# Three mixture-of-experts layers: routing joined to the experts, and token rows packed in 21 blocks instead of 24

## The reference, cut to what matters

```
logits = h @ w_group + b, h @ w_expert + b
group  = best of 4;  experts = best 2 of the 8 in it;  gates from both softmaxes
for each expert e, for the rows that chose it:
    y = (silu(x @ w_gate[e]) * (x @ w_up[e])) @ w_down[e]
out[token] = sum over its two rows of gate * y
```

## Time and profile before

| | us |
|---|---|
| median of 3 runs | 4115.12 (4114.41 to 4116.6) |
| the profiled execution, its own time | 4115.45 |
| its span from first to last instruction | 4113.5 |
| PE busy | 3484.4 (85%) |
| DVE, ACT, POOL busy | 1571.3, 873.8, 235.5 |
| bytes moved by DMA | 842.26 MB, 205 GB/s in the mean |

### The profile page before, as it was taken

One profiled execution on the slowest core, in us unless ns is written; L12 is line 12 of the kernel. 1 busy time (PEld: TensorE's weight loads), 2 busy tenths in 40 slices (PEclk: granted clock), 3 DMA queues, 4 the chain that ended last, 5 costly groups with the idle time before them and its releaser, 6 DMA issues. The chain is left out here.

```text
span 4113.5 us, 48036 instructions
## 1 busy us (share of the span) xinstructions
PE 3484.4 (85%) x18756; PEld 1936.0 (47%) x18756; DVE 1571.3 (38%) x2595; ACT 873.8 (21%) x1896; POOL 235.5 (6%) x250
## 2 busy tenths in 40 slices
PE   7998988499999598999874999985999657847994
PEld 3444644144444244777442444433556456425662
DVE  4641755200000674666452000004426673551114
ACT  0001721011111123555110101002335322001112
POOL 1002000200000100000002000001000000011001
PEclk9999998699999799999986999997999878968997
DMA  9963031599996610000316999956210310419994
GB/s 379 357 220 122 7 130 66 209 427 426 426 422 256 201 57 1 1 1 2 140 56 239 427 426 427 421 227 213 88 46 23 112 46 22 159 36 366 420 390 195
DMA packets 176908, 842.26 MB, mean 205 GB/s; under 512 B 53455, under 2 KB 60367, under 8 KB 130610
## 3 DMA queue, kind: packets, MB, share of 16 engines
q1 hardware_dynamic: 142434, 737.83, 44.8%
q0 software_dynamic: 20576, 54.16, 3.6%
q10 hardware_dynamic: 13680, 47.24, 2.9%
HBM read 758.39 MB, written 97.20 MB: 208 GB/s over the span
## 5 line engine op out<-in xcount | busy, mean ns | idle before, releaser
L395 PE MATMUL front_acc<-front_hT,front_wt 128*128 128x512 f32 x512 | 224.8, 601 | 5.5 <-DMA front_wt<-in_na_w_qkv 5.5
L1215 PE MATMUL n_acc<-n_wt,n_hT 128*128 128x512 f32 (+2 forms) x512 | 191.3, 531 | 0.7 <-ACT n_hT L1255 0.7
L201 DVE TENSOR_REDUCE gqa_top<-gqa_scores 128x1 f32<-128x1024 f32 x128 | 150.8, 1220 | 101.5 <-PE gqa_scores L149 101.5
L232 ACT ACTIVATE gqa_probs<-gqa_scores,gqa_top 128x1024 f32<-128x1024 f32 x128 | 142.5, 1113 | 168.2 <-DVE gqa_top L201 168.2
L2137 PE MATMUL m1x_gp<-m1x_w,m1x_xT 128*128 128x512 f32 (+1 forms) x512 | 171.9, 600 | 1.5 <-issue 0.7
L2137 PE MATMUL m0x_gp<-m0x_w,m0x_xT 128*128 128x512 f32 (+1 forms) x512 | 171.4, 599 | 1.5 <-issue 0.7
L2162 PE MATMUL m1x_yp<-m1x_w,m1x_hidT 128*128 128x512 f32 (+1 forms) x512 | 169.3, 594 | 2.1 <-ACT m1x_hidT L2223 2.1
L2162 PE MATMUL m0x_yp<-m0x_w,m0x_hidT 128*128 128x512 f32 (+1 forms) x512 | 169.3, 594 | 2.1 <-ACT m0x_hidT L2223 2.1
L2137 PE MATMUL m0x_up<-m0x_w,m0x_xT 128*128 128x512 f32 (+1 forms) x512 | 168.8, 593 | 0.0
L2137 PE MATMUL m1x_up<-m1x_w,m1x_xT 128*128 128x512 f32 (+1 forms) x512 | 168.8, 593 | 0.0
L913 PE MATMUL n_acc<-n_wt,n_hT 128*128 128x512 f32 x384 | 168.2, 598 | 0.7 <-ACT n_hT L931 0.7
(11 more groups left out here) (617 smaller groups left out, 5469.6 us busy)
## 6 DMA issues: line engine op xcount, KB each, us to landing
m0x_w<-in_moe_w_gate SPq DMA_DIRECT2D x32, 2048.0 KB, 33.3
m0x_w<-in_moe_w_up SPq DMA_DIRECT2D x32, 2048.0 KB, 33.2
m0x_w<-in_moe_w_down SPq DMA_DIRECT2D x32, 2048.0 KB, 33.4
m1x_w<-in_moe_w_gate SPq DMA_DIRECT2D x32, 2048.0 KB, 32.7
m1x_w<-in_moe_w_up SPq DMA_DIRECT2D x32, 2048.0 KB, 32.7
m1x_w<-in_moe_w_down SPq DMA_DIRECT2D x32, 2048.0 KB, 33.2
v<-in_ada_w SPq DMA_DIRECT2D x40, 1024.0 KB, 12.4
m2x_w<-in_moe_w_gate SPq DMA_DIRECT2D x32, 1024.0 KB, 32.2
```

What stands on the lines that cost most here:

```text
L201: dve.tensor_reduce(top[:, n % 2, h:h + 1], scores[h][:, :], AX.X, ALU.max, negate=True).then_inc(max_ready, 1)
L232: act.activation(probs[:, n % 2, h], scores[h][:, :], ACT.Exp, bias=top[:, n % 2, h:h + 1], accum_out=total[:, n % 2, h:h + 1]).then_inc(p ...
L395: last = pe.matmul(acc[n % 4][:, :], wt[:, c % 2, k, i * P:(i + 1) * P], hT[:, k, half * 512:(half + 1) * 512], start=k == 0, stop=k == KC ...
L1215: last = pe.matmul(acc[c][:, 0:n1 - n0], hT[:, t % 2, k], wt[:, k, n0:n1], start=k == 0, stop=k == KC - 1)
```

## The change

`route` and `experts` become one stage, `mixture`. What it does, part by part:

- Logits stay in SBUF (`keep["raw"]`); the store and the load go. Identity, router constants, token numbers and biases are loaded once, at the end of `front`, and stay; the identity loads in the other stages go. `tri`, `ones` and a new table `across` are loaded at the stage's start.
- Counts come from one reduction and two matmuls; experts are ranked with a 32 x 32 comparison; the list of experts by rank is a matmul (`plan_ps`), and SP starts the weights from it.
- The list of rows for the gathers is made on chip: a 2048-element comparison per partition on DVE, 16 matmuls that make a table (expert x position), and 8 matmuls that pick the blocks' columns out of it. The first two gathers are issued from it.
- The places of the rows in HBM (`place_rows`, 20 DVE operations up to `places`), the 16 indirect DMAs and the stores of places and gates remain, but now behind gathers 0 and 1 on POOL's queue and ahead of gather 2; on DVE they stand behind the first copy of the transposed rows. They serve overflow blocks and the next stage.
- Packing: the 16 smallest experts stay two to a block with 64 rows each (8 blocks). The next 12 (ranks 16 to 27) get 96 rows each: nine have a block's first 96 rows, and three are cut in pieces of 32 rows that fill the rest of three blocks each (9 blocks). The four largest have 128 (4 blocks). 21 blocks, and 22 in m2.
- A piece of 96 rows is done as 64 + 32, so in each of the nine blocks every step has three matmuls, with array tiles of 64, 32 and 32 columns, in that order.
- The weight ring of 10 slots becomes a table of 9 (18 in m2), each slot given to the matrix whose slot is free earliest; a cut expert's three matrices stay for three blocks.
- `SPILL_BLOCKS` goes from 16 to 21.

```diff
-SPILL_BLOCKS = 16
+SPILL_BLOCKS = 21
...
+        self.cap = [HALF_P] * SMALL + [96] * (LONE + SPLIT) + [P] * (R - top0)
+        self.cap[-1] += P * tops
...
+        pair = [(i, [(2 * i, 0, HALF_P), (2 * i + 1, HALF_P, HALF_P)]) for i in range(pairs)]
+        lone = [(pairs + i, [(SMALL + i, 0, 96), (split0 + i // SPLIT, 96, 32)]) for i in range(LONE)]
+        large = [(pairs + LONE + i, [(top0 + i, 0, P)]) for i in range(R - top0)]
...
+        def pieces(n):
+            out = []
+            for r, row, width in layout.blocks[n][1]:
+                while width:
+                    size = P if width == P else min(width, HALF_P)
+                    out.append((r, slice(row, row + size)))
+                    row, width = row + size, width - size
+            return out
...
                         for k in range(KC):
-                            for s, q in enumerate(qs):
-                                r = rows_of(n, s)
-                                last = pe.matmul(acc[r, 0:F], xT[:, j, k, r], w[:, q % RING, k * F:(k + 1) * F], start=k == 0, stop=k == KC - 1)
+                            for r, part in pieces(n):
+                                last = pe.matmul(acc[part, 0:F], xT[:, j, k, part], w[:, place_of[m_, r][0], k * F:(k + 1) * F],
+                                                 start=k == 0, stop=k == KC - 1)
...
+                pool.wait_ge(d, at["rows"])
+                gather(0)
+                gather(1)
+                pool.wait_ge(filled, 16)
+                pool.wait_ge(d, at["places"])
+                for k in range(2):
+                    for t in range(T):
+                        pool.indirect_dma_start(out=row_table, ...).then_inc(t_st, 16)
+                pool.dma_start(places, pu[:, :, :]).then_inc(out_st, 16)
+                gather(2)
...
+                choose()
+                rank_experts()
+                list_rows()
+                copy_x(dve, dve.tensor_copy, 0, 0)
+                place_rows()
+                weigh_rows()
+                product(0)
...
-                sp.wait_ge(l_cp, TILES)
-                sp.dma_start(rows(logits), lg[:, :, :]).then_inc(l_st, 16)
-                sp.wait_ge(l_st, 16)
```

More of the change, by code:

```diff
@@ L335, in _ @@
                 load_weights(5)
+                for tile, src in keep["loads"]:
+                    sp.dma_start(tile, src).then_inc(kept_in, 16)
+                sp.wait_ge(kept_in, 16 * len(keep["loads"]))
             @block.gpsimd
@@ new lines, with mixture @@
+SMALL = 16
+def mixture(nc, name, keep, bt, constants, h, wg, wu, wd, y, layer, row_table, places, gates, layout):
+    F = wg.shape[-1]
+    KC, FC = D // P, F // P
+    UNIT = KC * F
+    RING = layout.slots
+    G, E, T, X = N_GROUPS, PER_GROUP, TILES, N_EXPERTS
+    by_expert = lambda w: w.rearrange("l e (p c) f -> (l e) p (c f)", p=P)
+    sources = {"g": by_expert(wg), "u": by_expert(wu), "d": by_expert(wd)}
+    LAYERS_EXPERTS = wg.shape[0] * X
+    place_of, N, LISTED = layout.place, layout.N, layout.listed
+    ROWS = N + SPILL_BLOCKS
+    BASE = N * P
+    ident, cst, raw, tok_id = (keep[n] for n in ("ident", "cst", "raw", "tok_id"))
@@ new lines, in mixture @@
+        tri, ones, across = (sb(n, [P, P]) for n in ("tri", "ones", "across"))
+        empty = sb("empty", [P, ROW_BLOCKS], U32)
+        ri, rcol = sb("ri", [P, ROWS], U32), sb("rcol", [P, 1], U32)
+        x, xT = sb("x", [P, 2, D]), sb("xT", [P, 2, KC, P])
+        w = sb("w", [P, RING, UNIT])
+        sg, hid, hidT, yt = sb("sg", [P, 2, F]), sb("hid", [P, 2, F]), sb("hidT", [P, FC, P]), sb("yt", [P, 2, D])
+        at_pos = yt[:, :, :].rearrange("p e (n q) -> p (e n) q", q=P)
+        turn = [st.ps(f"turn{b}", [P, 512]) for b in range(2)]
@@ L1842, in _ @@
[L1842 to L1870, removed]
@@ new lines, in _ @@
+                for n_ in range(1, N):
+                    product(n_)
+                    if n_ + 1 < N:
+                        copy_x(dve, dve.tensor_copy, n_ + 1, 0)
+                    copy_y(dve, dve.tensor_copy, n_ - 1, 0)
+                copy_y(dve, dve.tensor_copy, N - 1, 0)
+                dve.sem_inc(so_y[0], 1)
+                spills = spilled(dve)
+                for j in range(2):
+                    dve.wait_ge(stored[j], 16 * ((N + 1 - j) // 2))
+                with dve.Fori(0, SPILL_BLOCKS) as i:
+                    with dve.If(i < spills):
+                        dve.wait_ge(so_t, i + 1)
+                        dve.tensor_copy(xT[:, 0, half[0]], turn[0][:, :].rearrange("p (c s) -> p c s", c=4)).then_inc(so_cp[0], 1)
+                        dve.wait_ge(so_sg, i + 1)
+                        dve.tensor_tensor(hid[:, 0], sg[:, 0], up[0][:, 0:F], ALU.mult).then_inc(so_hid, 1)
+                        dve.wait_ge(so_st, i * 16 + 16)
+                        dve.wait_ge(so_dn, i + 2)
+                        dve.tensor_copy(yt[:, 0, 0:512], yp[0][:, :]).then_inc(so_y[0], 1)
@@ L2150, in down @@
                 def down(n):
[L2151 to L2153 removed]
+                    arrived("d", n)
                     if n:
@@ L2983, in host_constants @@
     moe = [np.arange(N_GROUPS, 0, -1), np.arange(PER_GROUP, 0, -1), P * np.arange(TILES), np.arange(N_EXPERTS)]
-    moe = np.concatenate([np.tile(np.concatenate(moe), (P, 1)), part[:, None]], axis=1)
+    moe = [np.tile(np.concatenate(moe), (P, 1)), part[:, None], part[:, None] + P * np.arange(TILES)[None, :] - UNUSED_ROW]
+    for tops in range(2):
+        layout = Layout(tops, 18)
+        moe += [np.pad(np.array(v), (0, P - N_EXPERTS))[:, None] for v in (layout.start, layout.cap, layout.stair)]
+    moe = np.concatenate(moe, axis=1)
     return {
@@ L2999, in build, with stages @@
 def build(nc, a, out):
+    with ExitStack() as stack:
+        tile = lambda n, shape, dt=F32: stack.enter_context(nc.sbuf_tensor(f"keep_{n}", shape, dt))
+        keep = {"ident": tile("ident", [P, P]), "cst": tile("cst", [P, a["moe_const"].shape[1]]),
+                "tok_id": tile("tok_id", [P, TILES], U32), "raw": tile("raw", [P, TILES, N_GROUPS + N_EXPERTS]),
+                "bias": [tile(f"bias{i}", [P, N_GROUPS + N_EXPERTS]) for i in range(3)]}
+        stages(nc, a, out, keep)
+def stages(nc, a, out, keep):
     def scratch(name, *shape, dt=F32):
```

593 lines of the change are left out of this document (303 added, 290 removed).

## The result

The changed kernel takes **4531.95 us** (median of 4 runs, 4527.66 to 4533.83) against 4115.86 for the kernel before (4 runs, 4114.41 to 4117.07): ratio 1.1011, 95% interval 1.0997 to 1.1024. The forecast was 4497, so +382 against a measured +416. The profiled execution took 4527.66 us with a span of 4525.9, 4 us under the median.

What follows compares the result with a forecast made beforehand. PE was taken to bound the mixture stages, DMA just behind. m0 and m1 at -68 + 234 - 33 + 9 + 3 = +145 each and m2 at +92 gave +382 on 4115.4, about 4497 us; range 3890 to 4540.

Steps and rivals of the forecast that it cites:

- The mixed step: Nine mixed blocks: 64 then 32s, drained between, 1.94 us a step; +234 us in m0 and m1, +134 in m2; chance 0.62.
- Side by side: Rival, mixed blocks: 64- and 32-column pieces overlap, a step stays 0.86 us, DMA decides m0 and m1; 3923 us; chance 0.28.
- In turn without draining: Rival, mixed blocks: groups of 64 and 32 follow at the stream's pace, 1.72 us a step; 4360 us; chance 0.07.
- staggered: Rival, mixed blocks: each piece starts a pass after the one before, 1.29 us a step; about 4123 us; chance 0.03.
- Three blocks fewer: Blocks of each mixture stage: three fewer at an unchanged price save 68 us in m0 and m1, 36 in m2.
- The head: Stage start, logits to first product: the first product comes 32.8 us earlier, 30 in m2.
- Gather 2: After PE's first blocks: rows of gather 2, issued behind the scatters, come late; cost 9 us in m0 and m1, 21 in m2.
- The tail: Last store to next stage: five more empty turns of the overflow loop, +3 us a layer.

Runs made afterwards that it cites:

- e1: Changed kernel with a lone expert's 96 rows as three pieces of 32 columns instead of 64 + 32; 3943.04 us, 0.9581 of the kernel before.
- e2: Changed kernel with, in mixed blocks, all steps of the 64-column piece before all steps of the two 32s; 4382.79 us, ratio 1.0648.
- e6: Changed kernel without the third piece of each mixed block, leaving one tile of 64 and one of 32 columns a step; 4530.6 us, one run.
- e3: Changed kernel with the packing of the kernel before (no mixed blocks, 16 overflow turns); 4052.93 us, ratio 0.9848.
- e4: Changed kernel with gather 2 issued ahead of the 16 scatters; 4489.27 us.
- e5: Changed kernel with the 96 rows as three pieces of 32 and gather 2 ahead of the 16 scatters; 3945.52 us, ratio 0.958.
- e8: Changed kernel with pieces of 32 and the overflow loop inside one test, gather 2 behind the scatters; 3913.4 us, ratio 0.9507.
- e9: e8 with gather 2 first and the scatters spread, four ahead of each of gathers 3 to 6; 3891.23 us, ratio 0.9456.

## Why the prediction was right, and where its terms were off

**The mixed step** was the step that decided, and it held: forecast 1.94 us a step with bounds 1.90 and 1.98, measured 15.88 / 8 = 1.985. I had taken the middle; the upper end, two fenced groups of 0.99 as in the earlier trace rows, was the measurement. The e1 block of 22.9 against 49.7 makes +26.8 a block instead of +26.0, +241 instead of +234 in m0 and in m1. In m2 a gate step is 9.05 / 8 = 1.13 (forecast 1.09); with down 8.01 against 3.65 a block costs 2 x (9.05 - 3.51) + 4.36 = 15.4, nine +139 instead of +134. (By its own terms the forecast's width of 35 us for 1.90 to 1.98 a step is that of m0 and m1 alone; m2's 180 mixed steps add 14. And its 703 us of PE should be 477 + 234 = 711.) That nothing overlaps across widths, which the earlier trace rows showed only at hand-overs, e2 and e6 show inside a step. The Trainium skill (TensorEngine Tiling (Array Packing), section Key Properties) says that a change of tiling mode drains TensorE. The trace agrees, and adds the size, 0.11 to 0.13 us a change here, against 6.89 us a product for the lost overlap.

**Side by side**, the rival at 0.28, is refuted for unequal tiles and confirmed for equal ones: e1 lands at 3943 where that rival gave 3923, with the DMA engines as the limit, as it was worked out. The Trainium skill (TensorE: Matmul & The Clock Gate, section Measured speedup vs the span model) gives packed tiles the span of one matmul and some 4 ns for each further tile. For four tiles of 32 the trace agrees (6.89 us a product), for 64 beside 32 it doesn't (14.00 at best). **In turn without draining** would give 8 x 1.72 = 13.8 us a gate product and is refuted by 15.88, and by the 1.88 us between e2 and the changed kernel; **staggered** would give 10.3, and is refuted by 15.88 and by e6.

**Three blocks fewer**: -68 and -36 were right while PE ends the stage. With cheap mixed blocks they aren't: from e3 to e1 m0's part shortens by 1321.6 - 1278.6 = 43 us, or 46 with the 3.5 of five more turns taken off; about 22 of 68 are lost. Waits for weights are 13.3 of them, and the up products behind the two longest are 3.9 longer than usual (8.47 and 9.53 us for 7.05; granted clock 0.83 and 0.74). The two kernels' own difference doesn't see that.

**The head**: weights start at 722.65 (forecast 722.6). The list was there at 733.5 instead of 737.7, because the small float32 products were mis-sized, 10.8 us for 48 records: the 32 of the table took 5.54 us, 0.173 each, and the 16 that pick from it 1.0, lying side by side in the trace. So the first product came at 747.85 instead of 752.3, -37.1 instead of -32.8; in m2 (4005.71 - 3965.35 = 40.4 after the logits against 76.6) -36.2 instead of -30.

**Gather 2**: waits of 8.55 us in m0 and 17.7 in m2 against 9 and 21. Missing was what follows a pause: the next down product took 9.17 us instead of 7.03, 2.1 us more, at a granted clock of 0.76.

**The tail**: 3.7 us instead of 3.

In m0 the measured terms are -37.1 - 68 + 241 + 8.6 + 2.1 + 3.7 = +150 of 158. Another 1.6 us is the first product (10.13 against 8.54 us, at a granted clock of 0.70 in 748 to 758 us against 0.84 in 785 to 794), 2.6 the second block, whose gate and up products took 16.57 us in this execution and 13.95 in those of e2 and e4. Some 4 us are left, 2 of them because a mixed block is 27.0 us above the 22.7 of the kernel before. The layers of m0 and m1 were forecast 13 and 16 us short, m2 2 us: mixed blocks and slow starts were priced too low, and the head's gain too low as well, which partly cancels.

**Left open**: what holds ACT and DVE in m2 while the scatters run, and breaks the second up product in all three layers. The changed kernel and e5 to e8 show it, e1 to e4 don't with the same 16 scatters in a row, and e9 shows only part of it. The programs don't sort them: PE's is the same in e1 as in e5, those of the other engines in e4 as in e5. e1 to e4 ran on another chip than e5 to e9 (that of the changed kernel isn't on record); whether that is the cause, or the engines' code being fetched, or something else, no run here tells, and it wasn't tried. That DMA ends m0 and m1 in e1 is read from a share of 1.00 and from e5's early start that was lost again; a kernel with fewer bytes wasn't tried, and the 3.6 and 6.5 us that m0 and m1 gained in e9 aren't explained.

## What to carry to other kernels

Pack a PE array with tiles of one width: cut the wide piece to the narrow one's width, even if that makes more instructions (four tiles of 32 cost 6.89 us where 64, 32, 32 cost 15.88). If widths must be mixed, group them, but that buys only the drains. Before packing denser, see what bounds the stage once PE is faster, look at which transfers queue behind a burst of small ones, and put one test around a loop that is usually empty.

## What was not expected of the hardware

Sixty-four records with 32-column weights and 256 moved columns start within 3.48 us, one each 54 ns, with no sign of a limit on issuing them. An empty turn of a loop with one comparison costs 0.62 to 0.71 us, 13 us for 21 turns. And while POOL issues 16 indirect scatters, one each 1.27 us, ACT and DVE stop for 10 to 12 us in m2 of some runs and not in others that have the same scatters (e5 and e4), with no cause that the profile names.
